# The last quarter of V's columns as one dense product in a gated-mixer and expert layer: a table of weights in SBUF, and five V tiles beside each U block

## The chip, the cores and the metric

The kernel runs on 1 core of one Trainium2 chip. The metric is device microseconds of one execution. Of the kernel before there are three runs: 2294.17 us median, 2292.59 to 2314.82.

## What is computed

In short: one trunk layer for 256 prompt tokens and 8 sample tokens of width 2048, everything in float32. The first part projects the tokens by w_in, runs a gated linear attention and a short convolution, merges them and projects by w_out. The second part is the one that the change touches: 8 heads pick 16 of 16,384 experts for each token, and each picked expert is one neuron with a row of U and a row of V.

```python
q = (ht @ w_query).reshape(T, PEER_HEADS, 2, DQ_HALF)
s1 = einsum('thd,nd->thn', q[:, :, 0], sub_keys[0]); s2 = einsum('thd,nd->thn', q[:, :, 1], sub_keys[1])
v1, i1 = top_k(s1, 16); v2, i2 = top_k(s2, 16)
cand = v1[..., :, None] + v2[..., None, :]; cidx = i1[..., :, None] * 128 + i2[..., None, :]
top, pos = top_k(cand, 16); idx = take_along_axis(cidx, pos); g = softmax(top)
a = einsum('thkd,td->thk', expert_u[idx], x)            # rows of 2048 numbers
w = g * gelu(a)
out = einsum('thk,thkd->td', w, expert_v[idx])
y = rmsnorm(x + out)
```

U and V have 16,384 rows of 2048 numbers (8 KB) each. The 256 prompt tokens with 128 picks each ask for 32,768 rows of U and as many of V.

## The kernel before

Up to about 950 us the first part runs, bound by TensorE. Then comes the expert part, in which the work is cut into tiles of 128 rows (1 MB): 256 tiles of U, 256 of V, and 8 and 8 for the samples. A block is one head of one group of 128 tokens, 16 tiles of U (16 picks of 128 tokens); there are 16 blocks (`N_BLK`).

- **GpSimd** issues one indirect DMA per tile (`fetch`, L737) into a ring of 8 slots (`ring`, `RING`, 6 of them until the last queries are read), in the order of `order_of`: from block 1 on a U tile of block b and a V tile of block b-1 by turns. Before each it waits until the slot's last tile was used (`free_slot`).
- **VectorE** takes the dot product of each U tile with the tokens (`dot`, L1523, which leaves a weight per token), and between the dots of a block it does the retrieval of the next one: `keys_of` after dot 1, `pairs_of` after dot 4, `experts_of` after dot 7. `weights_of` multiplies the gelu by the shares. `widen`, `turned_idx` and `turned_w` turn a block's numbers of rows and weights, with one small product on TensorE each (`turn_z`), so that 16 tokens by 8 picks become the partitions of a V tile.
- **TensorE** weighs a V tile (`weigh`, L1988): four matmuls, one for each 512 columns, with stationary weights of 128 x 32 each, in four strips of 32 columns of the array. They run side by side and add up in PSUM bank `sum_bank(t, j)` for 32 tokens. In blocks 1 to 3 it also computes the queries that are left (`query`, L1942) and their scores (L1954).
- **ScalarE** does the exponentials, the gelu, and at the end the squares and roots of the last norm. **SyncE** loads w_query and stores the results.

All of V runs one block behind U, so that after block 15 of U there are 16 V tiles left alone.

## Time and profile before

| | |
|---|---|
| runs | 2292.59, 2294.17, 2314.82 us |
| span of the profiled execution | 2290.5 us |
| busy: TensorE, VectorE, ScalarE, GpSimd | 1601.0, 1319.7, 559.4, 708.7 us |
| read from HBM, written | 755.95 MB, 23.35 MB |

The span is the time from the first to the last instruction of the profiled execution. Its busy times are averages over a first part that TensorE fills and a second part in which the DMA engines are full; each has to be read from its own stretch. PEclk is the TensorE clock that was granted, as a share of 2.4 GHz. A wait names the instruction or the transfer that ended it.

### The profile page before, as it was taken

The numbers are of one execution on the slowest core, as the hardware profiler recorded it, in microseconds if no ns is written. First come the engines' busy times: TensorE is split into PE (matmuls) and PEld (weight loads), VectorE is DVE, ScalarE is ACT, GpSimd is POOL, SyncE is SP. The second block draws the span as 40 slices with busy tenths as digits, with TensorE's granted clock in tenths as the row PEclk, the third lists the DMA queues.
The fourth block names the chain that finished last, engine by engine and source line by source line (L and its number), as shares of the span: only waits on it lengthen the run. The fifth ranks groups of instructions, "written<-read, shape, count | busy, mean of one in ns | idle before, by whom it ended". The sixth has DMA issues, their size and how long they took to land.

```text
span 2290.5 us, 26072 instructions
## 1 busy us (share of the span) xinstructions
PE 1601.0 (70%) x10425; PEld 1087.3 (47%) x10425; DVE 1319.7 (58%) x2004; ACT 559.4 (24%) x773; POOL 708.7 (31%) x735
## 2 busy tenths in 40 slices
PE   9999999999999999967774444544443344444436
PEld 8999999999999999843441000100000000000001
DVE  6444556646555664685655665567566665465541
ACT  6333555545555543410000000000000000000000
POOL 1000110110111101354344444444435544344432
PEclk9999999999999999988886555555555555555555
DMA  9876878887878777799999999999999999999998
GB/s 251 226 192 194 238 227 241 247 247 215 252 210 246 226 221 225 270 418 426 423 427 422 427 427 427 427 427 427 427 426 426 426 427 427 427 427 427 428 427 337
DMA packets 435165, 780.93 MB, mean 341 GB/s; under 512 B 39640, under 2 KB 353904, under 8 KB 367200
## 3 DMA queue, kind: packets, MB, share of 16 engines
q0 software_dynamic: 89424, 597.80, 62.6%
q1 hardware_dynamic: 343904, 179.06, 28.5%
q10 hardware_dynamic: 1720, 2.44, 0.3%
q8 instruction: 82, 1.34, 0.2%
q14 instruction: 35, 0.29, 0.0%
HBM read 755.95 MB, written 23.35 MB: 340 GB/s over the span
## 4 chain that ended last, share of the span: by engine, by line
PE 46%; DMA 44%; DVE 6%; issue 2%; POOL 2%; ACT 1%; SPq 0%; POOLq 0%; ACTq 0%; DVEq 0%
DMA ring<-in_expert_v,idx_turned 22%; DMA ring<-in_expert_u,idx_all 19%; PE bank L1789 12%; PE bank L1790 12%; PE bank L1791 12%; DVE ring L1523 4%; PE bank L1988 3%; PE bank L1942 2%; POOL ring L737 2%; DMA ring<-in_expert_u,idx_s 1%; DMA ring<-in_expert_v,idx_s 1%; PE bank L1898 1%; PE bank L1879 1%; DMA x2T<-x_turned 0%; DMA x_tok<-in_x_prompt 0%
## 5 line engine op out<-in xcount | busy, mean ns | idle before, releaser
L1988 PE MATMUL bank<-ring,weigher 128*32 128x512 f32 x2048 | 461.7, 994 | 644.6 <-DMA ring<-in_expert_v,idx_turned 607.6
L1523 DVE CUSTOM_DVE_ANT_0 ring<-ring,xn_tok 128x2048 f32<-128x2048 f32 x256 | 586.0, 2291 | 456.4 <-DMA ring<-in_expert_u,idx_all 455.5
L1789 PE MATMUL bank<-act_hi,w_hi 128*128 128x264 f32 x2272 | 653.0, 287 | 0.4 <-DVE x2T L1373 0.4
L1790 PE MATMUL bank<-act_lo,w_hi 128*128 128x264 f32 x2272 | 643.8, 283 | 0.0
L1791 PE MATMUL bank<-act_hi,w_lo 128*128 128x264 f32 x2272 | 643.5, 283 | 0.0
L1988 PEld LDWEIGHTS bank<-ring,weigher 128*32 128x32 f32 x2048 | 50.7, 135 | 983.1 <-DMA ring<-in_expert_v,idx_turned 935.6
L1112 DVE TENSOR_TENSOR w_lo<-raw,w_hi 128x2048 fp32r<-128x2048 f32 x142 | 325.6, 2293 | 321.6 <-ACT w_hi L772 321.0
L1789 PEld LDWEIGHTS bank<-act_hi,w_hi 128*128 128x128 f32 x2272 | 427.9, 188 | 19.6 <-issue 19.2
L1790 PEld LDWEIGHTS bank<-act_lo,w_hi 128*128 128x128 f32 x2272 | 428.2, 188 | 1.7 <-issue 1.7
L1791 PEld LDWEIGHTS bank<-act_hi,w_lo 128*128 128x128 f32 x2272 | 426.0, 187 | 0.0
L737 POOL DMA_INDIRECT ring<-in_expert_u,idx_all x256 | 274.2, 1071 | 482.1 <-DVE w_all L1523 331.5
L737 POOL DMA_INDIRECT ring<-in_expert_v,idx_turned x256 | 308.5, 1205 | 296.3 <-PE bank L1988 231.8
L772 ACT ACTIVATE w_hi<-raw 128x2048 fp32r<-128x2048 f32 x142 | 272.1, 1916 | 417.7 <-PE bank L1791 413.4
L691 POOL DMA_DIRECT2D out<-s_ring x64 | 35.0, 547 | 496.3 <-DVE s_ring L1329 496.3
L1060 ACT ACTIVATE w_all<-w_all 128x16 f32<-128x16 f32 x16 | 3.5, 216 | 647.9 <-DVE w_all L1523 647.8
L1942 PE MATMUL bank<-h2T,wq 128*128 128x264 f32 x448 | 121.2, 432 | 0.0
L1942 PEld LDWEIGHTS bank<-h2T,wq 128*128 128x128 f32 x448 | 94.5, 216 | 39.4 <-issue 21.6
L1013 ACT ACTIVATE soft<-soft,rstd 128x16 f32<-128x16 f32 x16 | 4.9, 307 | 327.9 <-DVE soft L1429 327.8
L665 POOL DMA_DIRECT2D v_samples<-v_tok x1 | 0.8, 757 | 161.7 <-DVE v_tok L1237 161.7
L1969 PEld LDWEIGHTS bank<-div,widened 128*128 128x128 f32 x64 | 15.3, 297 | 69.0 <-issue 54.4
L994 ACT ACTIVATE q_s<-bank 128x8 f32<-128x8 f32 x16 | 2.8, 173 | 139.3 <-PE bank L1942 138.3
L676 POOL DMA_DIRECT2D s_ring<-in_state_gla x64 | 34.5, 540 | 3.2 <-issue 2.5
(331 smaller groups left out, 1169.9 us busy)
## 6 DMA issues: line engine op xcount, KB each, us to landing
raw<-in_w_in SPq DMA_DIRECT2D x129, 1024.0 KB, 6.9
s_ring<-in_state_gla POOLq DMA_DIRECT2D x64, 256.0 KB, 5.9
out<-s_ring POOLq DMA_DIRECT2D x64, 256.0 KB, 5.6
raw<-in_w_out SPq DMA_DIRECT2D x16, 1024.0 KB, 5.7
wq<-in_w_query SPq DMA_DIRECT2D x8, 2048.0 KB, 24.6
v_row<-v_samples POOLq DMA_DIRECT2D x32, 256.0 KB, 5.9
ring<-in_expert_u,idx_all POOLq DMA_INDIRECT x256, 17.0
ring<-in_expert_v,idx_turned POOLq DMA_INDIRECT x256, 17.3
```

The lines of the kernel that those rows point to most:

```text
L676: g.dma_start(s_ring[n % N_S][:], st_in[:, n // M, k, j, :]).then_inc(s_in[n % N_S], 16)
L691: g.dma_start(st_out[:, step // M, k, j, :], s_ring[step % N_S][:]).then_inc(s_out[step % N_S], 16)
L737: g.indirect_dma_start(ring[slot_of[n]][:], None, table, bass.IndirectOffsetOnAxis(ap=idx, axis=0)).then_inc(ring_in[slot_of[n]], 16)
L772: a.activation(w_hi[n0 % 2][:], raw[s][:], ACT.Copy).then_inc(hi_done, 1)
L1112: v.tensor_tensor(w_lo[n0 % 2][:], raw[s][:], w_hi[n0 % 2][:].bitcast(F32), ALU.subtract).then_inc(lo_done, 1)
L1523: v.tensor_tensor_reduce(ring[k][:], ring[k][:], xn_tok[:, b // PH, :], 1.0, 0.0, ALU.mult, ALU.add, w_all[:, b * TOPK + s:b * TOPK + s + ...
L1789: mm(out, hi_, act_hi[:, k, :], start=(k == 0), stop=False)
L1790: mm(out, hi_, act_lo[:, k, :], start=False, stop=False)
L1791: ins = mm(out, lo_, act_hi[:, k, :], start=False, stop=(k == KT - 1))
L1879: ins = mm(bank[KV0 + k][:], k_tok[:, k, :], v_, start=True, stop=True)
L1942: ins = mm(out, w[:, k, cols_], h2T[:, k, :], start=(k == 0), stop=(k == KT - 1))
L1988: ins = mm(bank[sum_bank(t, j)][c * STRIP:(c + 1) * STRIP, :], weigher[b % 2][:, s, :], ring[k][:, c * 512:(c + 1) * 512], start=False, st ...
```

## The change

The last 512 of V's 2048 columns are no longer gathered. A table `w_tab` in SBUF (128 partitions x 128 x 256 numbers, 128 KB of each partition) gets the weight of every expert for every token: partition b, position a holds expert 128a + b. Then the last quarter of all 16,384 V rows is read once, in 128 tiles of 128 x 512, and each is multiplied by the table for both groups of 128 tokens. The gathered V tiles have 1536 columns (6 KB in a row) now. The expert part has four stages:

- **U stage**: the 16 blocks of U. Beside each block from 1 on go five V tiles (`V_AT`), 75 in all.
- **Table stage**: 64 groups of 4 tokens (`N_GRP`). VectorE builds for each token two one-hot matrices, one of them times the weights (`one_hots`); TensorE multiplies them (`table`), ScalarE copies the product into `w_tab` (`table_out`). Between them TensorE weighs 53 V tiles (`mid_tiles`).
- **Dual stage**: 28 rounds of four V tiles and four or five dense steps (`dense`), 112 V tiles and 128 dense steps. SyncE loads the dense tiles into six slots (`dn`), GpSimd the V tiles into five (`v_slot`), since the table takes the ring's place.
- **Last block**: 16 V tiles. VectorE adds the dense sums of 512 columns to the rest (`merge`), then come the squares and the norm of both token groups. Before, the first group was normalised in block 9.

A V tile has three matmuls in three of the four strips. Which three changes from tile to tile (`strip_of`, `C_ORDER`, `row_of`). Semaphores of some other stages are put together into fewer ones, without another order of work.

```diff
+    ev_keys = expert_v.rearrange("o (a b) d -> b (o a) d", b=NKEY)
...
+        DENSE, SIDE = D // 4, 3 * (D // 4)
+        N_VS, N_DN, N_OH, GROUP = 5, 6, 2, 4
+        N_GRP = 2 * P // GROUP
+        w_tab = sb_at("w_tab", [P, NKEY, 2 * P], F32, at_act)
...
+        def strip_of(c, t, j):
+            return (c + 1 + j) % 4 if t < 2 else c
...
+        V_AT = (2, 5, 8, 11, 14)
+        N_V = N_BLK * TOPK
+        N_EARLY = (N_BLK - 1) * len(V_AT)
+        N_MID = N_V // 2
+        def early_v(b, s):
+            return divmod((b - 1) * len(V_AT) + V_AT.index(s), TOPK) if b > 0 and s in V_AT else None
+        def row_of(n, r):
+            return r if n == N_BLK - 1 else r % 4 * 4 + r // 4
+        C_ORDER = ((0, 1, 2), (2, 0, 1), (1, 2, 0), (2, 0, 1))
...
-        for g in range(N_BLK + 1):
+        for g in range(N_BLK):
             for s in range(TOPK):
-                if g < N_BLK:
-                    order_of.append((U_, g, s, "dot"))
-                if g > 0:
-                    order_of.append((V_, g - 1, s, "pe"))
+                order_of.append((U_, g, s, "dot"))
+                if early_v(g, s):
+                    order_of.append((V_, *early_v(g, s), "pe"))
                 if g == S_U and s % 2:
                     order_of.append((US_, 0, s // 2, "dot"))
                 if g == S_V and s % 2:
                     order_of.append((VS_, 0, s // 2, "pe"))
+        N_RING = len(order_of)
+        order_of += [(V_, *divmod(m, TOPK), "pe") for m in range(N_EARLY, N_V)]
...
-        z_order = [("idx", 0), ("idx", 1)]
-        for g in range(1, N_BLK + 1):
-            z_order.append(("w", g - 1))
-            if g + 1 < N_BLK:
-                z_order.append(("idx", g + 1))
+        z_order = [(kind, n) for n in range(N_BLK) for kind in ("idx", "w")]
...
+        def mid_tiles(g):
+            n = N_MID - N_EARLY
+            return range(N_EARLY + g * n // N_GRP, N_EARLY + (g + 1) * n // N_GRP)
+        N_DUAL = N_V - TOPK - N_MID
+        def dense_steps(q):
+            return range(q * NKEY * 4 // N_DUAL, (q + 1) * NKEY * 4 // N_DUAL)
...
+            for a in range(NKEY):
+                if a >= N_DN:
+                    sp.wait_ge(dn_used, a - N_DN + 1)
+                sp.dma_start(dn[a % N_DN][:], ev_keys[:, a, SIDE:D]).then_inc(dn_landed[a % N_DN], 16)
+            sp.wait_ge(dn_used, NKEY)
...
+            def fetch_late(n, r):
+                m = turn_of[V_, n, r]
+                k = late_slot(m)
+                if m < N_RING + N_VS:
+                    for old in {3: (), 4: (), 0: (3, 4), 1: (4, 5), 2: (5,)}[k]:
+                        who, count = done_at[last_in[old]]
+                        pool.wait_ge(u_used if who == "dot" else pe_used, count)
+                    if k >= 3:
+                        pool.wait_ge(u_used, eaten(US_, 0, PH - 1))
+                else:
+                    pool.wait_ge(pe_used, done_at[m - N_VS][1])
+                g.indirect_dma_start(v_slot[k][:], None, ev,
+                                     bass.IndirectOffsetOnAxis(ap=row_idx(n, r), axis=0)).then_inc(v_landed[k], 16)
...
+            def table_out(g):
+                act.wait_ge(w_mm, g + 1)
+                a.activation(w_tab[:, :, g * GROUP:(g + 1) * GROUP], bank[g % 2][:].rearrange("p (x i) -> p i x", x=GROUP),
+                             ACT.Copy).then_inc(w_built, 1)
...
+            def beside_v(n, r):
+                if n + 1 < N_BLK:
+                    if r == 8:
+                        widen_idx(n + 1)
+                    if r == 10:
+                        turned_idx(n + 1)
+                    if r == 12:
+                        widen_w(n + 1)
+                    if r == 14:
+                        turned_w(n + 1)
...
+            def one_hots(g):
+                t, at = g // (N_GRP // 2), g % (N_GRP // 2) * GROUP
+                if g % (N_GRP // 2) == 0:
+                    dve.wait_ge(pick_step, pick_count("ready", t))
+                if g >= N_OH:
+                    dve.wait_ge(w_mm, g - N_OH + 1)
+                shape = [P, GROUP, P]
+                v.tensor_tensor(oh1[g % N_OH][:], pick_T[t][:, 0, at:at + GROUP].unsqueeze(2).broadcast_to(shape),
+                                iota_key[:].unsqueeze(1).broadcast_to(shape), ALU.is_equal)
+                for x in range(GROUP):
+                    ins = v.tensor_scalar(oh2[g % N_OH][:, x, :], iota_key[:], pick_T[t][:, 1, at + x:at + x + 1],
+                                          pick_T[t][:, 2, at + x:at + x + 1], ALU.is_equal, ALU.mult)
+                ins.then_inc(oh_ready, 1)
+            def merge():
+                dve.wait_ge(dn_used, NKEY)
+                dve.wait_ge(y0_ready, 4)
+                for j in range(4):
+                    own_rows = slice(j * STRIP, (j + 1) * STRIP)
+                    v.tensor_tensor(y0_sb[own_rows, j, :], y0_sb[own_rows, j, :], bank[5][own_rows, :], ALU.add)
+                chained(v.tensor_copy(dn[0][:], bank[6][:]))
+                for j in range(4):
+                    own_rows = slice(j * STRIP, (j + 1) * STRIP)
+                    ins = v.tensor_tensor(bank[j][own_rows, :], bank[j][own_rows, :], dn[0][own_rows, :], ALU.add)
+                ins.then_inc(merged, 1)
...
+                for c in C_ORDER[j]:
+                    x = strip_of(c, t, j)
+                    ins = mm(bank[sum_bank(t, j)][x * STRIP:(x + 1) * STRIP, :], weigher[n % 2][:, s, :],
+                             rows[:, c * 512:(c + 1) * 512], start=False, stop=last)
...
+            def table(g):
+                pe.wait_ge(oh_ready, g + 1)
+                if g >= 2:
+                    pe.wait_ge(w_built, g - 1)
+                for x in range(GROUP):
+                    ins = mm(bank[g % 2][:, x * P:(x + 1) * P], oh2[g % N_OH][:, x, :], oh1[g % N_OH][:, x, :],
+                             start=True, stop=True)
+                ins.then_inc(w_mm, 1)
+            def dense(a):
+                if a == 0:
+                    pe.wait_ge(w_built, N_GRP)
+                    pe.wait_ge(y0_ready, 4)
+                pe.wait_ge(dn_landed[a % N_DN], 16 + 16 * (a // N_DN + 1))
+                for t in range(2):
+                    ins = mm(bank[5 + t][:], w_tab[:, a, t * P:(t + 1) * P], dn[a % N_DN][:], start=(a == 0),
+                             stop=(a == NKEY - 1))
+                ins.then_inc(dn_used, 1)
...
+                    if early_v(b, s):
+                        weigh(*early_v(b, s))
...
+            pe.wait_ge(s_step, S_PICKED)
+            for g in range(N_GRP):
+                if g == N_GRP // 2:
+                    turn_picks(1)
+                table(g)
+                for m in mid_tiles(g):
+                    weigh(*divmod(m, TOPK))
+            pe.wait_ge(w_built, N_GRP)
+            pe.wait_ge(x2b_ready, 1)
+            pe.wait_ge(pick_step, pick_count("ready", 1))
+            for q in range(N_DUAL // 4):
+                for m in range(N_MID + 4 * q, N_MID + 4 * q + 4):
+                    weigh(*divmod(m, TOPK))
+                for a in dense_steps(q):
+                    dense(a)
+            for r in range(TOPK):
+                weigh(N_BLK - 1, r)
+                if r == 5:
+                    y_totals(1, TILE_0)
+                if r in (6, 9, 13, 15):
+                    j = {6: 0, 9: 1, 13: 2, 15: 3}[r]
+                    y_totals(2 + j, [(1, j)])
...
```

GpSimd in the U stage, in the middle of the blocks; the DMA's slot stands left of the arrow. Before:

```order
L737 DMA ring_201<-in_expert_v,idx_turned 128x2048
L737 DMA ring_194<-in_expert_u,idx_all 128x2048
L737 DMA ring_195<-in_expert_v,idx_turned 128x2048
L737 DMA ring_196<-in_expert_u,idx_all 128x2048
L737 DMA ring_197<-in_expert_v,idx_turned 128x2048
L737 DMA ring_198<-in_expert_u,idx_all 128x2048
L737 DMA ring_199<-in_expert_v,idx_turned 128x2048
```

and now:

```order
L835 DMA ring_200<-in_expert_u,idx_all 128x2048
L835 DMA ring_201<-in_expert_v,idx_turned 128x1536
L835 DMA ring_194<-in_expert_u,idx_all 128x2048
L835 DMA ring_195<-in_expert_u,idx_all 128x2048
L835 DMA ring_196<-in_expert_u,idx_all 128x2048
L835 DMA ring_197<-in_expert_v,idx_turned 128x1536
L835 DMA ring_198<-in_expert_u,idx_all 128x2048
L835 DMA ring_199<-in_expert_u,idx_all 128x2048
```

U and V alternated; now a V tile, of 1536 columns, stands after every third or fourth U tile.

VectorE at the end of the U stage and in the first groups of the table stage (`oh` are the one-hot matrices, `pick_T` the keys and weights with the tokens in the columns). Nothing of this stood there before:

```order
L1732 TENSOR_TENSOR w_all<-w_all,g_all 128x16
L1740 TENSOR_SCALAR key_num<-idx_all 128x128
L1741 TENSOR_SCALAR key_num<-idx_all 128x128
L1742 CAST key_val<-key_num 128x256
L1752 TENSOR_TENSOR oh_0_233<-pick_T_223,iota_key 128x512
L1755 TENSOR_SCALAR oh_0_235<-iota_key,pick_T_223 128x128 x4
L1752 TENSOR_TENSOR oh_1_234<-pick_T_223,iota_key 128x512
L1755 TENSOR_SCALAR oh_1_236<-iota_key,pick_T_223 128x128 x4
L1752 TENSOR_TENSOR oh_0_233<-pick_T_223,iota_key 128x512
L1755 TENSOR_SCALAR oh_0_235<-iota_key,pick_T_223 128x128 x4
L1686 TENSOR_TENSOR widened_late_226<-w_all,mod_165 128x128
```

Each group has one operation of 512 columns and four of 128 ahead of TensorE's four matmuls, and what turns the next V block's weights stands between the groups.

TensorE near the middle of V before (`ring` is a V tile, L1969 turns numbers of rows or weights):

```order
L1988 MATMUL bank2<-ring3_197,weigher0_181 32x512 x4
L1988 MATMUL bank3<-ring5_199,weigher0_181 32x512 x4
L1988 MATMUL bank3<-ring7_201,weigher0_181 32x512 x4
L1988 MATMUL bank3<-ring1_195,weigher0_181 32x512 x4
L1988 MATMUL bank3<-ring3_197,weigher0_181 32x512 x4
L1969 MATMUL bank7<-div8_166,widened0_184 128x16
```

In the table stage now (`oh1`, `oh2` are multiplied into the table, `v_slot` is a V tile, L2187 is `turn_z`):

```order
L2253 MATMUL bank0<-oh1_0_233,oh2_0_235 128x128 x4
L2253 MATMUL bank1<-oh1_1_234,oh2_1_236 128x128 x4
L2220 MATMUL bank7<-v_slot1_217,weigher0_181 32x512 x3
L2253 MATMUL bank0<-oh1_0_233,oh2_0_235 128x128 x4
L2220 MATMUL bank4<-v_slot2_218,weigher0_181 32x512 x3
L2253 MATMUL bank1<-oh1_1_234,oh2_1_236 128x128 x4
L2187 MATMUL bank3<-div8_166,widened_late0_225 128x16
```

And in the dual stage (`dn` is a dense tile, `w_tab` the table):

```order
L2264 MATMUL bank5<-dn3_230,w_tab_215 128x512
L2264 MATMUL bank6<-dn3_230,w_tab_215 128x512
L2220 MATMUL bank0<-v_slot0_216,weigher0_181 32x512 x3
L2220 MATMUL bank1<-v_slot1_217,weigher0_181 32x512 x3
L2220 MATMUL bank2<-v_slot2_218,weigher0_181 32x512 x3
L2220 MATMUL bank3<-v_slot3_219,weigher0_181 32x512 x3
L2264 MATMUL bank5<-dn4_231,w_tab_215 128x512
L2264 MATMUL bank6<-dn4_231,w_tab_215 128x512
L2264 MATMUL bank5<-dn5_232,w_tab_215 128x512
L2264 MATMUL bank6<-dn5_232,w_tab_215 128x512
```

TensorE weighed one V tile after another and waited for each. Now a group of the table stands ahead of nearly every V tile, and later nine or ten products of 128 x 128 x 512 behind every four V tiles; the four V tiles go to four banks.

## Rows read from the trace of the kernel before

**Rows 1.** The page: the span, and GB/s in 40 slices of 57.3 us.

```profile
span 2290.5 us, 26072 instructions
...
GB/s 251 226 192 194 238 227 241 247 247 215 252 210 246 226 221 225 270 418 426 423 427 422 427 427 427 427 427 427 427 426 426 426 427 427 427 427 427 428 427 337
```

**Rows 2.** The page: the chain that ended last, by engine and by line.

```profile
PE 46%; DMA 44%; DVE 6%; issue 2%; POOL 2%; ACT 1%; SPq 0%; POOLq 0%; ACTq 0%; DVEq 0%
DMA ring<-in_expert_v,idx_turned 22%; DMA ring<-in_expert_u,idx_all 19%; PE bank L1789 12%; PE bank L1790 12%; PE bank L1791 12%; DVE ring L1523 4%; PE bank L1988 3%; PE bank L1942 2%; POOL ring L737 2%; DMA ring<-in_expert_u,idx_s 1%; DMA ring<-in_expert_v,idx_s 1%; PE bank L1898 1%; PE bank L1879 1%; DMA x2T<-x_turned 0%; DMA x_tok<-in_x_prompt 0%
```

**Rows 3.** Windows: stretch, length, engines busy us (count), PEclk, DMA share, GB/s.

```profile
1045.00:1065.00 20.00, 14.34 (x80) 8.56 (x80) 12.97 (x26) 1.05 (x3) 10.42 (x8) 0.93 1.01 427
1240.00:1280.00 40.00, 16.78 (x70) 2.11 (x66) 24.14 (x42) 1.50 (x2) 18.36 (x17) 0.50 1.01 427
1520.00:1560.00 40.00, 15.82 (x70) 2.10 (x66) 29.03 (x70) 1.59 (x2) 15.30 (x17) 0.50 1.01 426
1560.00:1600.00 40.00, 18.03 (x78) 3.05 (x70) 27.92 (x57) 3.09 (x4) 19.00 (x17) 0.50 1.01 429
```

**Rows 4.** Waits of 1240 to 2240 us: engine, line, releaser, us, times, longest.

```profile
PE bank L1988 <- DMA ring<-in_expert_v,idx_turned: 539.2, 180, 6.3
DVE ring L1523 <- DMA ring<-in_expert_u,idx_all: 367.3, 153, 5.1
```

**Rows 5.** The page: DMA queues, packets, MB, share of 16 engines.

```profile
q0 software_dynamic: 89424, 597.80, 62.6%
q1 hardware_dynamic: 343904, 179.06, 28.5%
```

**Rows 6.** Tile ring: GpSimd issues (ns, min/median/max) and us to landing.

```profile
L737 POOL DMA_INDIRECT ring<-in_expert_v,idx_turned x256: 935/939/3041, 999.7 to 2264.4; - x128
...
DMA to landing us min/median/max: 5.8/17.0/21.3
```

**Rows 7.** VectorE's timeline: start, us, line, operation, names, shapes, idle time before.

```profile
1528.70 0.25 DVE L1436 CAST key_f<-key_u 128x16 f32<-128x16 uint32 x2
...
1532.63 0.29 DVE L1538 TENSOR_TENSOR widened<-idx_f,mod 128x128 f32<-128x128 f32 x1
1532.83 2.28 DVE L1523 CUSTOM_DVE_ANT_0 ring<-ring,xn_tok 128x2048 f32<-128x2048 f32 x1
...
1578.62 0.48 DVE L1392 MAX8 val<-sc 128x8 f32<-128x128 f32 x2
...
1581.62 2.29 DVE L1523 CUSTOM_DVE_ANT_0 ring<-ring,xn_tok 128x2048 f32<-128x2048 f32 x1
...
1593.32 0.42 DVE L1423 TENSOR_TENSOR cand<-val 128x256 f32<-128x256 f32 x1
...
1596.38 2.28 DVE L1523 CUSTOM_DVE_ANT_0 ring<-ring,xn_tok 128x2048 f32<-128x2048 f32 x1
```

**Rows 8.** TensorE's timeline: the same columns; each fp32 matmul leaves two records.

```profile
1051.52 1.07 PE L1988 MATMUL bank<-ring,weigher 128*32 128x512 f32 x8
1052.40 1.04 PE L1976 MATMUL bank<-x_tok,ident 128*32 128x512 f32 x8
...
1075.32 3.83 PE L1942 MATMUL bank<-h2T,wq 128*128 128x264 f32 x16
...
1091.89 1.16 PE L1954 MATMUL bank<-keysT,stage 128*128 128x128 f32 x8 [0.54 <-ACT stage L996]
1092.98 1.06 PE L1988 MATMUL bank<-ring,weigher 128*32 128x512 f32 x8
...
2246.68 3.64 PE L1988 MATMUL bank<-ring,weigher 128*32 128x512 f32 x16 [0.78 <-DVE weigher L1556]
```

**Rows 9.** Groups by line from 1000 us: count, busy us, mean ns, idle.

```profile
L1556 DVE TENSOR_TENSOR weigher<-bank,own 128x512 f32<-128x512 f32 x16 | 11.0, 686 | 1.9 <-PE bank L1969 1.9
...
L1538 DVE TENSOR_TENSOR widened<-w_all,mod 128x128 f32<-128x128 f32 x16 | 4.7, 292 | 0.5
...
L1009 ACT ACTIVATE sc<-bank 128x512 f32<-128x512 f32 x5 | 3.0, 598 | 6.5 <-PE bank L1954 6.5
```

More of the change, by code:

```diff
@@ L65, in hybrid_step @@
     STRIP = 32
[L66 removed]
+    N_CONSTS, N_LATE_CONSTS = 25, 13
     N_LINKS = 18
@@ L115, in hybrid_step @@
         ident = sb("ident", [P, P])
+        at_causal = where[0]
         causal = sb("causal", [P, P])
@@ L215, in hybrid_step @@
         at_h2T = at_head + 2112
+        at_spread = where[0]
         spread = sb("spread", [P, P])
@@ L243, in hybrid_step @@
         picks = sb("picks", [P, 2, TOPK])
+        at_wide = where[0]
         wide = sb("wide", [P, 2, PH, TOPK])
@@ L757, in _ @@
                         fetch(ev, VS_, 0, s // 2, idx_s[:, s // 2:s // 2 + 1])
+            for m in range(N_EARLY, N_V):
+                n, r = divmod(m, TOPK)
+                if r == 0:
+                    pool.wait_ge(z_read, nth_z("idx", n) + 1)
+                fetch_late(n, r)
         @block.scalar
```

417 lines of the change are left out of this document (255 added, 162 removed).

## The prediction

> **What bounds the kernel now.** I read the chain of waits first [rows 2]: up to slice 16 of the page it runs through the projection's matmuls (L1789 to L1791), and all that lies behind belongs to the transfers of U and V. The reader should next look at GB/s [rows 1]: from slice 18 on it stands at 418 to 428, and the windows [rows 3] say that the 16 DMA engines have no idle time there, while TensorE is busy for 16.8 of 40 us and VectorE for 24.1. The waits [rows 4] agree: both engines wait for U and V tiles alone. So in the expert part only bytes and packets count, and a second question follows: which engine would be the next bound. At 427 GB/s a tile of 1,048,576 bytes takes 2.456 us. From block 1 on there are 240 tiles of U, 256 of V and 16 of the samples: 512 x 2.456 = 1257 us.
>
> **The price of a packet.** No tile has rows of 6 KB or 2 KB now, so I take a line through the two queues [rows 5]. q0: 62.6% of 16 x 2290.5 us over 89,424 packets is 256.5 ns for 6685 bytes in the mean; q1: 30.4 ns for 521 bytes. That is 11.3 ns and 36.7 ps for each byte: 311.8 ns for 8 KB, 236.7 for 6 KB, 86.4 for 2 KB. Scaled to the 2.456 us, a V tile now takes 1.864 us and a dense tile 0.681. All V tiles save 256 x 0.592 = 151.6 us, the dense tiles add 128 x 0.681 = 87.2. **If the DMA stayed the bound everywhere, that would be 64 us less.** By bytes alone (a dense tile 0.614 us, a V tile 1.842) it would be 79; with all dense tiles at q1's 17 GB/s an engine, 0.96 us, only 29. The rest of the sum is what the new stages give back.
>
> **U stage.** DMA: 256 x 2.456 + 75 x 1.864 = 769 us from block 1 on, for one block 16 x 2.456 + 5 x 1.864 = 48.6. VectorE must now fit its block into those 48.6 us instead of 78.6: 16 dots of 2.30 [rows 7], `keys_of` 3.0 (1578.62 to 1581.62), `pairs_of` 3.1, `experts_of` 4.1 less 0.25 that moves away, gelu and weights some 0.6, and 5/16 of the turning (about 1.75 a V block by the small rows [rows 7, 9]) 0.55: 47.8 us, 98% of the block. The ordinary blocks fit; the samples' retrieval adds some 9 us (VectorE is busy 29.0 and 27.9 of 40 us there instead of 24.1 [rows 3]). A ring of 8 absorbs about that: a tile lands 17.0 us after its issue against 5.8 at least [rows 6], so some 11 us are reserve. I take 5 us for lumps. To enter the table stage TensorE waits for the last dot, the gelu, `keys_in_halves` and the first group: 7 us, in which V's five and the dense six slots fill.
>
> **Table stage.** TensorE in a group: four fp32 matmuls of 128 columns took 1.09 us at full clock (1091.89 to 1092.98) [rows 8]. V tiles: 0.83 a group; a tile back to back took 0.88 us (1051.52 to 1052.40). Three strips instead of four cost no less when a product of the whole array follows: 0.88. That is 1.82 us a group, 117 us for 64, with the turning 118. VectorE: one operation of 512 columns is 0.69 busy, a 128 wide one 0.29 alone and 0.20 when another follows [rows 7, 9]: 1.4 to 1.85, I take 1.5 (the next one does follow). ScalarE: 0.60. DMA: 53 x 1.864 = 99 us. TensorE sets it, VectorE stands close behind.
>
> **Dual stage.** A dense step is two fp32 matmuls of 512 columns: 264 columns took 0.479 us (3.83 for 8), of which 0.44 are columns at 1.67 ns; 512 make 0.89, and 0.93 by proportion. So 4.57 x 1.78 = 8.1 us a round. Four V tiles: 3.5 us at 0.88, 2.6 if the changing strips really overlap (12 matmuls on 4 strips, three deep, 0.85 each). TensorE: 10.7 to 11.7 us a round; DMA: 4 x 1.864 + 4.57 x 0.681 = 10.6. Neither has room: TensorE takes V in bursts, so the five slots are asked for again within 3 us and the first data come 3.3 us after an issue (5.8 less a transfer of 2.46 [rows 6]). I take 11.4 us a round, 319 us.
>
> **Last block**: 5 of 16 tiles are there, 11 x 1.864 = 20.5 us, and 4.5 for `merge` and the norm of both groups, on whose sums `weigh` waits in rows 5 and 6 (nine VectorE operations and four squares come before it). 25 us, plus 4 for the seams before it and the end.
>
> **Sum**: 769 + 5 + 7 + 118 + 319 + 25 + 4 = 1247 us against 1257: **10 us less**. The profiled span becomes 2280.5; the median run stands 3.7 above that span, so I say **2284 us**, 0.4% below 2294.17.
>
> **The clock.** At PEclk 0.50 all these matmuls take twice as long: two V tiles took 3.64 us at 2246.68 [rows 8]. It stood at 0.50 while TensorE was busy 16.8 of 40 us, and at 0.93 while busy 14.3 of 20 [rows 3]. In both new stages it is busy over 90%, so I count with 2.4 GHz. The Trainium skill (TensorE: Matmul & The Clock Gate, "What's actually happening") says that the low clock is the default and activity lifts it; by that rule, the trace agrees.
>
> **Rivals.**
> - *The DMA stays the bound* (25%). It needs V tiles at 0.64 by overlapping strips and VectorE below 1.5 a group. Then: 769 + 5 + 7, table 64 x (1.09 + 0.53) = 104, dual 28 x 10.6 = 297, end 26: 1208 us, 49 less, 2245 us. For it: the four strips of a tile do run side by side [rows 8]. Against: nothing here shows two tiles at once.
> - *The dual stage starves* (18%). TensorE does its dense steps while V's slots fill and then waits for dense tiles that V held up. It ends above before by 1% when a round passes 12.6 us (11.4 + 33/28); at 13.0 it costs 45 us more: 2329 us. For it: eleven slots hold less than one and a half rounds, where before 8 tiles stood against one. Against: SyncE's dense loads need no GpSimd.
> - *VectorE overruns the U stage* (5%): at 51 us a block 15 x 2.4 = 36 us more, 2320 us. Against: all its parts have rows.
> - *GpSimd's issues are held up in the table stage* (5%). An issue took 0.94 us at the median and 3.04 at most [rows 6]. At 3.04 each the 53 tiles take 161 us instead of 118: 43 more, 2327 us. Against: 0.94 is also the median beside VectorE's dots. The Trainium skill (SBUF — State Buffer, "Who interferes with whom") says that a tensor_scalar in a two-port mode blocks GpSimd fully for its duration; four such stand in each group.
> - *The clock falls in the dual stage* (2%): a round of over 20 us, 250 us more, about 2530. Against: the windows above.
> - My forecast holds 45%, its own range 2264 to 2305.
>
> **How the numbers follow.** Faster by over 1% (below 2271; about what a measurement can tell from no change): the first rival, 24%, and 9% of my own case: 33%. Slower by over 1% (above 2317): the other rivals, 26%, and 2% of mine: 28%. Within: 39%. The range reaches to the first rival and to the starving round: 2245 to 2328.
>
> **What would show it.** GB/s near 425 through the U stage, about 353 in the table stage (53 x 0.786 MB in 118 us) and 381 in the dual stage. In the U stage VectorE over 95% busy, its waits for U tiles a tenth of those before. Table stage near 118 us, PEclk near 1. Dual stage: `dense` pairs of 1.78 us, a round of 11.4, both engines over 90%. Wrong if a V tile takes under 0.7 us between others, if matmuls wait for `dn` or `v_slot` more than 1.5 us a round, or if the DMA falls below 400 GB/s in the U stage's blocks 1 to 6.

## The result, and the profile after

The change makes the kernel **slower by 0.45%**: 2303.51 us median of 20 runs (2299.42 to 2307.33) against 2292.38 of 20 runs of before, ratio 1.0045 with a 95% interval of 1.0037 to 1.0053. The profiled execution has a span of 2300.1 us, 9.6 more than before's. I had forecast 10 us less.

The page of the changed kernel: span; busy; PEclk; GB/s; queues (packets, MB, share of 16 engines); what was read and written; the chain by engine.

```profile
span 2300.1 us, 27728 instructions
...
PE 1720.8 (75%) x10943; PEld 1231.2 (54%) x10943; DVE 1426.1 (62%) x2339; ACT 600.7 (26%) x843; POOL 892.2 (39%) x736
...
PEclk9999999999999999989855555555555799999998
...
GB/s 253 221 193 195 240 227 236 247 245 214 254 215 251 218 224 211 307 416 413 412 414 418 427 401 392 427 427 426 427 427 426 334 321 353 377 375 375 376 376 323
...
q0 software_dynamic: 89424, 530.69, 57.6%
q1 hardware_dynamic: 362912, 213.41, 32.5%
...
HBM read 723.19 MB, written 23.35 MB: 325 GB/s over the span
...
PE 61%; DVE 21%; DMA 9%; POOL 6%; issue 2%; ACT 1%; POOLq 0%; ACTq 0%; DVEq 0%
```

32.8 MB fewer are read. Against [rows 1] GB/s still stands at 412 to 427 in most slices up to the 31st, and falls to 320 to 377 from the 32nd on, where the table and dual stages begin. The exceptions are the 24th and 25th slice, at 401 and 392: from 1350 to 1400 us VectorE was busy for 48.6 of 50 us beside 383 GB/s, and that block took 57.3 us. Against [rows 2] the chain has turned round: DMA 9% instead of 44%, TensorE 61% instead of 46%, VectorE (DVE) 21% instead of 6%. The windows show the same by stage (columns as in [rows 3]): a block of the U stage, the table stage, the dual stage, the last block.

```profile
1240.00:1280.00 40.00, 11.96 (x30) 2.44 (x30) 37.90 (x66) 1.50 (x2) 31.84 (x18) 0.50 1.01 427
...
1811.00:1931.00 120.00, 117.67 (x804) 67.87 (x803) 105.99 (x319) 36.91 (x62) 49.58 (x50) 0.98 0.89 318
1945.00:2255.00 310.00, 308.98 (x1165) 114.90 (x1164) 10.23 (x33) 0.00 (x0) 100.52 (x108) 1.00 0.99 375
2263.00:2294.00 31.00, 20.91 (x101) 4.36 (x95) 11.84 (x24) 6.82 (x19) 10.37 (x11) 0.78 0.97 361
```

In the U stage the DMA moves what it moved before (427 GB/s), while VectorE's 24.1 of 40 us became 37.9, GpSimd's 18.4 became 31.8, and TensorE's 16.8 became 12.0. In the dual stage TensorE is busy for 309 of 310 us while the DMA moves 375 GB/s.

**Stages against the forecast.** The stages are cut at the end of the last dot and at the starts of the first and last table product, the last dense product and the last V tile.

| stage | forecast | measured | if the DMA set it, at my prices |
|---|---|---|---|
| U, entry | 781 | 780.8 | 778 |
| table | 118 | 126.8 | 98.8 |
| dual | 319 | 327.6 | 296 |
| last block | 29 | 32.1 | 20.5 |
| sum | 1247 | 1267.3 | 1193 |

The 778 are my 769 and 9.3 for the five V tiles that land before the table stage. For U, 799.1 us were measured (796.1 and 3.0 of entry), less 18.3 that I take as carried by both kernels: before took 1275.3 us from the first dot of block 1 (1009.1) to its last V tile, where my tiles gave 1257. Most of it lies in blocks 1 and 2, beside the late queries: 86.6 and 84.1 us before against 78.6 by my prices, 57.4 and 54.5 now against 48.6. Block 1 began 0.8 us earlier, the end took 0.1 more: 1267.3 - 1257 - 0.8 + 0.1 = 9.6. **So by my prices the DMA work shrank by 64 us, and the stages gave back 74**: 3 in U and entry, 28 in the table stage, 32 in the dual stage, 12 in the last block (rounded).

The table stage on TensorE's timeline (columns as in [rows 8]; L2253 is a table group, L2220 a V tile, L2187 a turn), its start, its end and the head of the dual stage (L2196 starts tile 1's sums), then two rounds of it (L2264 is dense):

```profile
1807.38 3.75 PE L2253 MATMUL bank<-oh,oh 128*128 128x128 f32 x16 [5.81 <-DVE oh L1755]
1811.06 1.90 PE L2220 MATMUL bank<-v_slot,weigher 128*32 128x512 f32 x6
...
1926.93 1.16 PE L2253 MATMUL bank<-oh,oh 128*128 128x128 f32 x8
1928.02 1.06 PE L2220 MATMUL bank<-v_slot,weigher 128*32 128x512 f32 x6
1929.00 1.16 PE L2253 MATMUL bank<-oh,oh 128*128 128x128 f32 x8
...
1935.15 1.15 PE L2196 MATMUL bank<-x2b,ident 128*32 128x512 f32 x8
...
1941.40 4.99 PE L2264 MATMUL bank<-dn,w_tab 128*128 128x512 f32 x11
...
2006.17 1.06 PE L2220 MATMUL bank<-v_slot,weigher 128*32 128x512 f32 x6
2007.16 0.40 PE L2187 MATMUL bank<-div,widened_late 128*128 128x16 f32 x2
2007.49 2.76 PE L2220 MATMUL bank<-v_slot,weigher 128*32 128x512 f32 x18
2010.18 8.85 PE L2264 MATMUL bank<-dn,w_tab 128*128 128x512 f32 x20
```

A table group takes 1.09 us as forecast, a V tile between two of them 0.98 to 0.99 (1928.02 to 1929.00) where I had 0.88. The first two groups run at the low clock (PEclk 0.50, 1.2 GHz, until 1812.8): 3.68 us instead of 2.18. Ten dense products take 8.8 us. Four V tiles with a turn among them take 4.01 us (2006.17 to 2010.18).

### The profile page after: what moved, and what is told of

Read it like the earlier page. It is cut to its first block, busy times and chain, and to the rows that moved or that the text cites. A ratio compares the mean times of both kernels' runs of the same rounds, so it can differ in the third digit from the quotient of the medians.

```text
span 2300.1 us, 27728 instructions
## 1 busy us (share of the span) xinstructions
PE 1720.8 (75%) x10943; PEld 1231.2 (54%) x10943; DVE 1426.1 (62%) x2339; ACT 600.7 (26%) x843; POOL 892.2 (39%) x736
## 4 chain that ended last, share of the span: by engine, by line
PE 61%; DVE 21%; DMA 9%; POOL 6%; issue 2%; ACT 1%; POOLq 0%; ACTq 0%; DVEq 0%
DVE ring L1672 14%; PE bank L2007 12%; PE bank L2008 12%; PE bank L2009 12%; PE bank L2264 9%; PE bank L2220 6%; DMA ring<-in_expert_u,idx_all 6%; POOL ring L835 5%; PE bank L2253 3%; DMA v_slot<-in_expert_v,idx_turned 2%; PE bank L2160 1%; DMA ring<-in_expert_v,idx_turned 1%; DVE key_u L1547 1%; PE bank L2116 1%; DVE pos L1547 1%
## 5 line engine op out<-in xcount | busy, mean ns | idle before, releaser
L1672 DVE CUSTOM_DVE_ANT_0 ring<-ring,xn_tok 128x2048 f32<-128x2048 f32 x256 | 577.6, 2287 | 61.4 <-DMA ring<-in_expert_u,idx_all 58.9
L835 POOL DMA_INDIRECT ring<-in_expert_u,idx_all x256 | 451.1, 1762 | 274.0 <-DVE w_all L1672 128.0
L2220 PE MATMUL bank<-ring,weigher 128*32 128x512 f32 x450 | 137.4, 1010 | 484.1 <-DMA ring<-in_expert_v,idx_turned 484.1
L2007 PEld LDWEIGHTS bank<-act_hi,w_hi 128*128 128x128 f32 x2272 | 428.0, 188 | 19.3 <-issue 18.9
L2220 PEld LDWEIGHTS bank<-ring,weigher 128*32 128x32 f32 x450 | 14.5, 136 | 579.9 <-DMA ring<-in_expert_v,idx_turned 538.7
L855 POOL DMA_INDIRECT v_slot<-in_expert_v,idx_turned x181 | 175.4, 969 | 319.0 <-PE bank L2220 287.6
L2264 PE MATMUL bank<-dn,w_tab 128*128 128x512 f32 x512 | 227.2, 598 | 0.0
L2220 PE MATMUL bank<-v_slot,weigher 128*32 128x512 f32 x1086 | 176.5, 618 | 9.3 <-DMA v_slot<-in_expert_v,idx_turned 9.3
L2264 PEld LDWEIGHTS bank<-dn,w_tab 128*128 128x128 f32 x512 | 95.0, 190 | 132.5 <-issue 132.5
L835 POOL DMA_INDIRECT ring<-in_expert_v,idx_turned x75 | 134.4, 1792 | 29.9 <-issue 20.7
L2160 PE MATMUL bank<-h2T,wq 128*128 128x264 f32 x448 | 109.4, 404 | 0.0
```

What stands on the lines that cost most here:

```text
L835: g.indirect_dma_start(ring[slot_of[n]][:, 0:width], None, table, bass.IndirectOffsetOnAxis(ap=idx, axis=0)).then_inc(ring_in[slot_of[n]], 16)
L855: g.indirect_dma_start(v_slot[k][:], None, ev, bass.IndirectOffsetOnAxis(ap=row_idx(n, r), axis=0)).then_inc(v_landed[k], 16)
L1672: v.tensor_tensor_reduce(ring[k][:], ring[k][:], xn_tok[:, b // PH, :], 1.0, 0.0, ALU.mult, ALU.add, w_all[:, b * TOPK + s:b * TOPK + s + ...
L2007: mm(out, hi_, act_hi[:, k, :], start=(k == 0), stop=False)
L2160: ins = mm(out, w[:, k, cols_], h2T[:, k, :], start=(k == 0), stop=(k == KT - 1))
L2220: ins = mm(bank[sum_bank(t, j)][x * STRIP:(x + 1) * STRIP, :], weigher[n % 2][:, s, :], rows[:, c * 512:(c + 1) * 512], start=False, stop= ...
```

## Experiments

Single executions of one kernel differ by up to 22 us, and so does the U stage, though it is the same program in several of them: with five V tiles a block it took 796.1 to 800.3 us in six kernels, with four 766.0 to 774.8 in five of the six that move the turns, and 788.3 in the sixth. The table stage repeats within 1 us where its program is the same, the dual stage within some 3. So effects are read from the stage first. U here counts from 1008.3 us, within 0.5 us of block 1's first dot in every kernel, and includes the 18.3 us; 3.0 us of entry follow it.

| kernel | median | ratio to before (95%) | U | table | dual | last | end |
|---|---|---|---|---|---|---|---|
| after | 2303.51 | 1.0045 (1.0037 to 1.0053) | 796.1 | 126.8 | 327.6 | 32.1 | 6.2 |
| a1_one_scaled | 2303.07 | 1.0045 (1.0028 to 1.0061) | 800.2 | 124.0 | 325.8 | 32.3 | 6.3 |
| a2_dense_half | 2272.56 | 0.9919 (0.9903 to 0.9936) | 797.9 | 126.3 | 294.1 | 33.3 | 6.4 |
| a3_turns_first | 2296.1 | 1.0017 (1.0008 to 1.0027) | 795.6 | 125.8 | 319.4 | 31.6 | 6.5 |
| a4_four_beside | 2292.53 | 0.9997 (0.9978 to 1.0016) | 768.6 | 141.9 | 328.9 | 33.0 | 6.6 |
| c1_four_turns | 2287.91 | 0.9987 (0.9971 to 1.0003) | 767.6 | 141.4 | 322.1 | 33.0 | 6.2 |
| c2_picks_early | 2283.66 | 0.9968 (0.9942 to 0.9994) | 774.8 | 138.3 | 320.1 | 32.0 | 6.1 |
| c3_short_last | 2288.29 | 0.9995 (0.9976 to 1.0014) | 772.7 | 138.5 | 332.3 | 15.4 | 18.9 |
| d1_three_beside | 2304.92 | 1.0053 (1.0039 to 1.0068) | 759.6 | 163.7 | 330.3 | 32.2 | 6.1 |
| e1_no_starts | 2279.97 | 0.9957 (0.9937 to 0.9978) | 773.0 | 139.0 | 320.8 | 31.5 | 6.6 |
| e2_stores_held | 2285.14 | 0.9963 (0.9948 to 0.9977) | 788.3 | 138.1 | 319.1 | 28.7 | 15.2 |
| e3_bursts_one_scaled | 2307.65 | 1.0087 (1.0057 to 1.0118) | 800.3 | 118.4 | 331.0 | 32.2 | 6.0 |
| e4_bursts_held | 2309.97 | 1.0085 (1.0056 to 1.0114) | 766.0 | 154.0 | 329.2 | 29.4 | 15.2 |
| f1_no_starts_after | 2302.93 | 1.0040 (1.0030 to 1.0049) | 800.1 | 126.5 | 326.5 | 31.4 | 6.0 |
| f2_whole_fours | 2307.07 | 1.0059 (1.0040 to 1.0079) | 798.5 | 124.2 | 332.4 | 32.4 | 6.5 |

### Who sets the table stage: a1_one_scaled

```diff
-                for x in range(GROUP):
+                for x in range(GROUP if g < N_OH else 1):
                     ins = v.tensor_scalar(oh2[g % N_OH][:, x, :], iota_key[:], pick_T[t][:, 1, at + x:at + x + 1],
```

> Leaves out three of the four scaled one-hot matrices of each group in the table stage (their buffers keep old numbers), so VectorE has about 0.8 us less work per group and TensorE, ScalarE and the transfers have the same. If VectorE sets the table stage (2.0 us a group in the changed kernel), a group falls to TensorE's 1.82 us or less and the whole is 11 to 15 us faster, near 2290. If TensorE or the V transfers set it, nothing moves (within 2 us).

VectorE's busy time in the stage fell by 46 us, from 111.0 to 64.6, the stage by 2.8. VectorE does not set it, beyond those 3 us; TensorE does.

### Who sets the dual stage: a2_dense_half

```diff
-                for t in range(2):
+                for t in range(2 if a in (0, NKEY - 1) else 1):
                     ins = mm(bank[5 + t][:], w_tab[:, a, t * P:(t + 1) * P], dn[a % N_DN][:], start=(a == 0),
```

> Leaves out one of the two products of 126 of the 128 dense steps; the dense tiles and the V tiles are still transferred. If TensorE sets the dual stage (11.6 us a round), it falls to the transfers' 10.6 us a round or a little over: 20 to 28 us faster. If the five V slots and the six dense slots set it (transfers that start too late), nothing or less than 8 us is gained.

The window of its dual stage:

```profile
1945.00:2225.00 280.00, 232.66 (x924) 68.90 (x923) 10.23 (x33) 0.00 (x0) 100.65 (x108) 0.96 1.03 415
```

33.5 us less, at 415 GB/s, and TensorE now waits for V and dense tiles. So TensorE set the stage. 294.1 / 28 = 10.5 us is the most that the DMA needs for a round; I had 10.6 from the two packet prices, whose sum is herewith borne out.

### The turns inside the bursts: a3_turns_first

```diff
-                    if r == 8:
+                    if r == 7:
...
-                    if r == 12:
+                    if r == 11:
...
-                if r == 9 and n + 1 < N_BLK:
+                if r == 8 and n + 1 < N_BLK:
...
-                if r == 13 and n + 1 < N_BLK:
+                if r == 12 and n + 1 < N_BLK:
```

> The two small turning products of each V block move from the middle of a burst of four V tiles (ahead of tiles 9 and 13) to its start (ahead of tiles 8 and 12), with VectorE's part one tile earlier. In the changed kernel a burst with a turn takes 4.07 us and one without 2.78. If the broken overlap of the strips is what costs, each of the 14 turns of the dual stage gets about 0.95 us cheaper: 11 to 14 us faster. If the turn itself (0.39 us) is the cost, or the stage waits for transfers, under 3 us.

TensorE's timeline with the turn ahead of the burst:

```profile
2003.24 0.29 PE L2187 MATMUL bank<-div,widened_late 128*128 128x16 f32 x2
2003.46 2.78 PE L2220 MATMUL bank<-v_slot,weigher 128*32 128x512 f32 x24
2006.17 8.85 PE L2264 MATMUL bank<-dn,w_tab 128*128 128x512 f32 x20
```

A turn and four V tiles take 2.93 us (2003.24 to 2006.17) instead of 4.01; 14 such places in the dual stage, 15 us on TensorE. The stage became 8.2 us shorter and the median 7.4: the DMA (383 GB/s now) stands close behind and took the rest, for TensorE's weight loads waited 11.8 us for V tiles instead of 6.2, and its products 3.4 instead of 1.0.

### Fewer V tiles beside U: a4_four_beside, d1_three_beside, and with the turns, c1_four_turns

```diff
-        V_AT = (2, 5, 8, 11, 14)
+        V_AT = (3, 7, 11, 15)
```

This is a4 and, on a3, c1. d1 has (4, 9, 14), and takes the second pair of turning buffers from block 3 on.

> Four V tiles beside each U block instead of five: 60 early ones instead of 75, and 68 in the table stage instead of 53. If VectorE sets the U stage (about 49 us a block whatever goes beside it), the U stage keeps its length within 8 us, and the total rises by what 15 more V tiles cost the table stage, 0 to 13 us. If the DMA sets the U stage, it gets 25 to 28 us shorter and the total falls by 10 or more.

> Three V tiles beside each U block instead of five (45 early, 83 in the table stage), nothing else. From five to four the U stage fell by 27.5 us, the time of 15 V tiles. If the transfers still set it, it falls by as much again, to 741 us; if VectorE is now the limit (it was busy 94 to 98% with four), by under 12 us. The table stage grows by about 15 us either way (83 V tiles are 155 us of transfers), so the total is 0 to 15 us slower than with four, or 12 faster.

> Four V tiles beside each U block and the turning products at the start of a burst, together. If the two act in different stages (U stage and dual stage), their gains add up: 11 + 7, so about 2285, 18 us under the changed kernel and 7 under the kernel before. If they share one limit (the transfers of the whole), the sum stays under 13, at 2290 or above.

Fifteen V tiles fewer shorten the U stage by 27.5 us (1.83 each; forecast 1.864; by the scatter above another pair of executions could give 21 to 34) and lengthen the table stage by 15.1 (1.01 each): where the DMA is the bound a V tile costs its transfer, where TensorE is, its 0.99 us. Another fifteen fewer (d1) shorten U by 9 only and lengthen the table stage by 21.8. The window of 1240 to 1280 us, with four and with three:

```profile
1240.00:1280.00 40.00, 14.77 (x32) 3.10 (x32) 39.30 (x60) 4.84 (x8) 32.38 (x18) 0.50 1.01 422
```

```profile
1240.00:1280.00 40.00, 10.02 (x19) 2.70 (x20) 39.28 (x60) 3.13 (x6) 30.45 (x17) 0.50 0.96 383
...
1775.00:1935.00 160.00, 151.53 (x1013) 76.97 (x1013) 111.45 (x335) 37.53 (x64) 80.08 (x81) 0.99 0.97 387
```

VectorE is full in both (39.3 of 40): about 46 us a block are its floor, and with three tiles the DMA runs empty beside it. In the table stage of d1 83 V tiles take 163.7 us, 1.97 each. By the prices TensorE needs 64 x 1.09 + 83 x 0.99 = 152 of them and the DMA 83 x 1.864 = 155; TensorE's weight loads wait 17.4 us for V tiles and 18.2 for one-hots. Which of the three sets that stage isn't shown. c1 adds a3's edit to a4's; the gains add up in the stages (767.6 and 322.1).

### The stall in the middle of the table: c2_picks_early

```diff
-                if g == N_GRP // 2:
+                if g == 4:
                     turn_picks(1)
```

On c1; the same on ScalarE for `picks_out(1)`.

> As c1_four_turns, and the second group's keys and weights are turned in group 4 of the table stage instead of group 32, where VectorE waited 4.0 us for ScalarE's copy and TensorE 1.6 us for VectorE. If that seam costs TensorE what it shows, 2 to 4 us faster than c1_four_turns; if VectorE has caught up with it again by the stage's end, no change.

The table stage went from 141.4 to 138.3, and VectorE's wait of 5.4 us for the second group's keys and weights is gone from the trace. c2_picks_early is **faster than before by 0.3%** (0.06 to 0.58), the best of the kernels that leave nothing out together with e2 below, which equals it. Its 10 executions lie between 2276.9 and 2299.35, so its own distance from c1 isn't shown by the medians.

### Fewer tiles behind the dual stage: c3_short_last

```diff
-        N_DUAL = N_V - TOPK - N_MID
+        N_DUAL = N_V - 8 - N_MID
```

On c2: eight V tiles are left for the last block, and all `y_totals` stand behind them.

> As c2_picks_early, and 8 of the last block's 16 V tiles go into two more rounds of the dual stage (30 rounds); the totals of the norm come after the last V tile. If a V tile costs 0.7 to 0.9 us of TensorE's time there and the last block is bound by its transfers and stores (32 us), the dual stage gets 6 us longer and the end 12 to 16 us shorter: 6 to 10 us faster than c2_picks_early, about 2274. If the chain of merge and norm (not the transfers) sets the end, it gets no shorter: same or 6 us slower.

The last block fell from 32.0 to 15.4 and more than that came back: the dual stage has two more rounds (+12.2) and the end grew by 12.8. So the work behind V's last tile grows when fewer V tiles cover it; how it divides among merge, squares, roots and stores was not taken apart.

### The stores in the last block: e2_stores_held

```diff
+            m = turn_of[V_, N_BLK - 1, TOPK - 1]
+            sp.wait_ge(v_landed[late_slot(m)], STATE_MOVES + 16 * ((m - N_RING) // N_VS + 1))
             for nth in range(1, N_SUM):
```

On c2.

> On c2_picks_early. The stores of tile 0's rows wait until the last V tile has landed; nothing else is changed. Theory A: in the last block the V tiles land every 2.33 us instead of 1.87 because these stores (1 MB in 64 KB pieces) share the DMA engines: the stretch from the last dense product to the last V tile, 32.0 us, comes down by 2 to 3, the tail of 6.1 grows by 0 to 1, and the time is 2281 to 2282. Theory B: the loads of the norm's weights or the merge set the last block: 32 stays, and the time is 2283.7 or up to 2.5 later, since the stores now lie in the tail.

The last block lost 3.3 us and the end grew by 9.1. So the stores do take time from V's last tiles, but are better there than behind them. (Its profiled execution was the slowest of its seven, with a U stage 14 us longer than that of c2; its table and dual stages are c2's within 1 us.)

### The products that start tile 1's sums: e1_no_starts, f1_no_starts_after

```diff
-                if n % PH == 0 and r < 4:
+                if t == 0 and n % PH == 0 and r < 4:
                     begin_sum(t, j)
```

This is e1 on c2, f1 on the changed kernel.

> On c2_picks_early. Left out: the sixteen products with the identity that start tile 1's sums from the residual (the first weighed tile of each strip starts its sum instead), so the output lacks that residual for tile 1. The wait for the last table groups and the copies of tile 0's sums beside them stay. Theory A: these products are plain TensorE time at the head of the dual stage, where the changed kernel took 6.2 us for them and four V tiles that otherwise take 2.8: from the last table product to the last dense product 320.1 us comes down by 3 to 3.5, and the time with it, 2283.7 to about 2280.5. Theory B: what is waited for there is the end of the table (ScalarE's copies) or the first dense tiles, and the products lie beside it: under 1 us.

> The changed kernel, with only the sixteen products left out that start tile 1's sums from the residual (the output lacks that residual for tile 1). With four V tiles beside each U block, as e1_no_starts has it, the table stage moves 375 GB/s and keeps the DMA engines 98% busy, and the products lay beside the landing of V tiles: there TensorE waited 4.6 us more for V tiles and the dual stage stayed at 320.8 us. Here the table stage keeps the engines 89% busy and the slots are full when it ends. Theory A: the products cost their TensorE time, 6.2 us against 2.8 for four V tiles: dual stage 327.6 becomes 324, the time 3.5 less than the changed kernel's, 2300. Theory B: also here V tiles land too late behind them: 327 and 2303.

At the head of the dual stage the changed kernel needs 6.2 us for a first burst that takes 2.7 later, and sixteen products stand in it. I took them for the cause. TensorE without them, in f1:

```profile
1938.10 3.10 PE L2221 MATMUL bank<-v_slot,weigher 128*32 128x512 f32 x18
1942.04 1.06 PE L2221 MATMUL bank<-v_slot,weigher 128*32 128x512 f32 x6 [0.84 <-DMA v_slot<-in_expert_v,idx_turned]
1943.93 1.06 PE L2221 MATMUL bank<-v_slot,weigher 128*32 128x512 f32 x6 [0.83 <-DMA v_slot<-in_expert_v,idx_turned]
1944.92 7.13 PE L2265 MATMUL bank<-dn,w_tab 128*128 128x512 f32 x16
```

6.8 us, now with waits for V tiles. The dual stage is 1.1 us shorter in f1 and 0.7 longer in e1, within their scatter. (e1's median is 3.7 us below c2's, as my theory had it, but c2's ten executions spread over 22 us.) My theory fell: without the products TensorE waits there for V tiles, which until then were used one by one; the products lie in that wait.

### What makes a V tile's price: e3_bursts_one_scaled, f2_whole_fours, e4_bursts_held

```diff
-            return range(N_EARLY + g * n // N_GRP, N_EARLY + (g + 1) * n // N_GRP)
+            return range(N_EARLY + (g - 3) * n // N_GRP, N_EARLY + (g + 1) * n // N_GRP) if g % 4 == 3 else ()
```

> On a1_one_scaled (three of four scaled one-hot tables left out, so the table of weights isn't the reference's; it takes VectorE away as a bound). The 53 V tiles of the table stage stand in bursts of three or four behind every fourth group, in place of one behind nearly every group. Theory A: a V tile alone between table groups costs TensorE 0.99 us because its strips can't overlap another tile's; in a burst it costs 0.70. The table stage, 124.0 us, comes down to 64 x 1.09 + 53 x 0.70 + some 3 of stall = 110, the time from 2303 to about 2290. Where the DMA binds first (53 tiles at 1.864 to 2.03 us) it is 105 to 110 as well. Theory B: a V tile costs the same wherever it stands: 124 stays, or grows by 1 to 3 where five slots are too few for a burst.

> On a1_one_scaled (three of four scaled one-hot tables left out). As e3_bursts_one_scaled, but the bursts of the table stage begin at tiles 76, 80, 84 ..., so each holds the four column orders once, as the bursts of the dual stage do. In e3_bursts_one_scaled three tiles took 2.7 us and four 3.7. Theory A: what counts is how the 128x32 products fill the four column strips in the order written: twelve products of four tiles in whole rounds of four strips take three rounds, 2.70 us, as in the dual stage; four tiles from another start take four rounds. Each burst takes 2.7, TensorE's work in the stage is 64 x 1.09 + 13 x 2.70 + 0.99 = 106, and the stage ends between 109 and 118, by how far five slots starve. Theory B: the table groups beside them set the price: bursts of four stay at 3.7 and the stage at 118 or more.

> On e2_stores_held: its 68 V tiles of the table stage stand in bursts of four or five behind every fourth group. Theory A (the DMA sets this stage with 68 tiles: 98% busy at 375 GB/s, 2.03 us a tile): 138.3 us stays within 2, and the time is that of e2_stores_held. Theory B (TensorE sets it, 0.99 us a tile against 0.70 in a burst): the stage comes down to the floor of VectorE's one-hots, 64 x 2.05 = 131, and the time by 7. Against both: bursts starve on five slots and the stage grows by some us.

(f2's bursts begin at tiles 76, 80, 84 ...) TensorE in e3, from 1861.05 to 1865.00:

```profile
1861.05 2.77 PE L2220 MATMUL bank<-v_slot,weigher 128*32 128x512 f32 x18
1864.02 1.06 PE L2220 MATMUL bank<-v_slot,weigher 128*32 128x512 f32 x6 [0.20 <-DMA v_slot<-in_expert_v,idx_turned]
1865.00 4.25 PE L2253 MATMUL bank<-oh,oh 128*128 128x128 f32 x32
```

and in f2:

```profile
1880.51 2.78 PE L2222 MATMUL bank<-v_slot,weigher 128*32 128x512 f32 x24
1883.22 3.36 PE L2255 MATMUL bank<-oh,oh 128*128 128x128 f32 x24
```

Four tiles in 3.95 us with 0.20 of wait, against four in 2.71, the figure of the dual stage. The table groups beside them are the same. I took the start of the burst for the difference: `strip_of` and `C_ORDER` give the strips 1 2 3, 0 2 3, 0 1 3, 2 0 1 for four tiles from a multiple of four on, and read strictly in this order they fill three rounds of four strips, but four rounds from any other start. The traces speak against it. In e4 a burst that begins at tile 81 takes 2.72 us:

```profile
1834.17 2.79 PE L2222 MATMUL bank<-v_slot,weigher 128*32 128x512 f32 x24
1836.89 1.27 PE L2255 MATMUL bank<-oh,oh 128*128 128x128 f32 x9
```

and in e3 one that begins at tile 84, a multiple of four, takes 3.54 (PEld is a weight load):

```profile
1838.62 3.62 PE L2220 MATMUL bank<-v_slot,weigher 128*32 128x512 f32 x24
1841.18 0.15 PEld L2220 LDWEIGHTS bank<-v_slot,weigher 128*32 128x32 f32 x6 [0.69 <-DMA v_slot<-in_expert_v,idx_turned]
1842.17 0.38 PE L2253 MATMUL bank<-oh,oh 128*128 128x128 f32 x1
```

What e3's three bursts of four without a turn have in common is a late fourth tile: its weight load waited 0.69 to 1.10 us for the transfer. Three tiles take 2.69 us, and the late one a round by itself. f2's bursts of four without a turn took 2.71 where all tiles were there, and 3.83 and more where some were late. Its 2.71 fits both accounts, so f2 did not decide between them; e4 does, with one burst.

All the prices fit rounds of 0.86 to 0.89 us, in each of which a strip does one product, and a gap before a product of the whole array. A tile alone is one round (0.99). Three tiles are three rounds, since one strip is used by each of them (2.69), and four tiles are three as well, since every strip is used by three of them (2.71). A turn closes the round: behind the first tile it makes 0.99 + 0.33 + 2.69 = 4.01.

Between the strips the written order is not kept. In e3's burst of the tiles 111 to 113, with strips 2 0 1, 1 2 3, 0 2 3, four products start at 1901.06, four at 1901.95 and one at 1902.81; in the written order it would be three, four and two. A tile's semaphore step stands on the last product of its code; the records with the steps of tiles 111 and 112 start at 1901.53 and 1901.55, and the one of tile 113 at 1902.41, before the last product. The Trainium skill (TensorE: Matmul & The Clock Gate, "Step-by-step: what each phase is for") says that matmuls stay in the order of the program and only weight loads are pulled ahead; across column strips these traces do not agree.

Bursts bring no time: against a1, on which both stand, the table stage became 5.6 us shorter in e3 and none in f2, and the dual stage 5 to 7 longer. TensorE is done sooner with a burst, but the slots are then asked for together and the last tile lands late; f2 waits for one-hots and V tiles in turn (`DMA v_slot` 9.7 us of the wait of its weight loads). With 68 tiles (e4, against e2) bursts cost 16 us in the table stage and 10 in the dual stage. Not tried was a greater number of slots, for which the table leaves no room.

## Why the prediction was wrong

**Right.** The DMA prices: a V tile beside U is 1.83 us (1.864), and a round of the dual stage 10.5 at most (10.6). U and entry 780.8 against 781, closer than the scatter of that stage lets one claim. VectorE is 95% busy in the U stage (37.9 of 40) and just fits there. The dense pair is 1.76 us (1.78), the clock full in both new stages but for the first 5 us (0.98, 1.00), and neither `dn` nor `v_slot` is waited for over 1.5 us a round: in the whole dual stage TensorE's products wait 1.0 us and its weight loads 6.2, all for `v_slot`. GB/s came out at 375 for 381 in the dual stage, but 318 for 353 in the table stage.

**Wrong, in sizes: 20.5 us in three terms**, which the U stage (0.2) and the start and end (0.7) softened to 19.6.

- *The table stage, 8.8 us.* The step that failed is "three strips instead of four cost no less when a product of the whole array follows: 0.88". It was taken from V tiles back to back [rows 8], where the next tile follows into strips that come free; ahead of a product of the whole array the tile costs 0.99. 53 x 0.11 = 5.8 us. The low clock over the first two groups and the first V tile adds 2.3 (5.5 us instead of 3.2), the wait for `turn_picks(1)` 2.3, the turns about 1 more than I had; as the last group and its V tile lie behind the cut (2.1) and the small terms are rounded, 8.8 are left. No row of [rows 8] has a tile ahead of such a product, so 0.88 was a lower bound and no price. VectorE's `tensor_scalar` took 0.26 us each in a run of four (1903.07 to 1904.10) and not 0.20, with an effect of 3 us at most (a1).
- *The dual stage, 8.6 us.* My round of 11.4 us, the middle between 10.7 and 11.7, came out, but by luck: it was 8.0 dense, 2.7 for four V tiles, and 1.3 for every second burst, in which a turn stands. The overlap of strips, which I gave to a rival, was there; the turns, which I had seen in the table stage's order and not looked for here, took it back. a3 shows their place to be worth 7.4 us of the time. The step that failed is that the sum gave neither the stage's head nor late V tiles any time: up to the first dense product the stage took 7.2 us, with five V tiles and the starts of tile 1's sums, where a burst takes 2.7, and five of the 27 later bursts were 0.6 to 1.1 us too long, 4.3 in all.
- *The last block, 3.1 us.* 3.3 are the stores of tile 0 (e2), which the DMA work of that block lacked in my sum.

The direction hung on 10 us between two sums of 1250, and the three terms that missed were all too small: two where TensorE sets the pace, one where the DMA does.

**The rivals.** *The DMA stays the bound*: no. Its first condition nearly held in the dual stage (0.68 us a V tile in a burst without a turn, for 0.64), but not in the table stage (0.99); its second did not (VectorE was busy 1.73 us a group, for 1.5). Even with a3's edit the dual stage took 319.4 / 28 = 11.4 us a round against a2's 10.5. *The dual stage starves*: no. *VectorE overruns the U stage*: no; plain blocks took 47 to 51 us. *GpSimd is held up in the table stage*: no, its 52 issues there have a median of 986 ns and took 1402 at most; the Trainium skill's rule on tensor_scalar, named beside that rival, shows in no number of that stage. *The clock falls*: no.

**Where the expected gain went.** A V tile's transfer was made cheaper, but in the last 500 us TensorE has 126.8 + 327.6 us of its own work where the DMA would need 98.8 by its price and 294 by a2. The bytes saved there were no longer the bound.

## What to carry over

When a kernel that is full on one resource trades it for work on others, add up each new stage by its own engine and look for what breaks that engine's best pace at every place, small products of another shape above all; a middle between two bounds hides them. Give a transfer to the stage in which it is cheapest: here a V tile cost 1.83 us beside U and 1.0 beside the table, until VectorE's floor (below four a block) and a longer table stage (at 83 tiles) turned that round. And price an operation by its neighbours: a V tile of three strips took 0.68 us among three others and 0.99 before a product of the whole array.
